# Squared-ReLU MLP jobs in pairs: products of two jobs alternate, quads kept twice, refill subtractions split between two engines

## What is computed

```python
hn = rms_norm(h, mlp_norm[i])
h = h + jnp.square(jax.nn.relu(hn @ w_mlp_in[i])) @ w_mlp_out[i]
```

## Time and profile before

| what | value |
|---|---|
| median of 3 runs | 2522.27 us (2521.65 to 2526.93) |
| the profiled execution's own time | 2522.98 us |
| its span, first to last instruction | 2521.2 us |
| granted TensorE clock, mean over the span | 0.966 |
| busy: TensorE, VectorE, GpSimd, ScalarE | 92%, 64%, 42%, 39% |
| MLP stages (line 1099) | from 542.9 and from 1699.4 us, some 675 us each |

### The profile page before, as it was taken

How to read it: one execution, slowest core, us unless ns; L and a number is a source line. 1 busy time by engine, 2 the same in 40 slices (tenths; PEclk the granted TensorE clock), 3 DMA queues, 4 the chain that set the end, 5 groups by cost and what they waited for, 6 DMA issues and landing times.

```text
span 2521.2 us, 31322 instructions
## 1 busy us (share of the span) xinstructions
PE 2321.1 (92%) x12286; PEld 1858.2 (74%) x12286; DVE 1611.7 (64%) x1959; ACT 980.9 (39%) x1526; POOL 1066.9 (42%) x684
## 2 busy tenths in 40 slices
PE   8998967997999989999998999987999989999997
PEld 6887856776888877777786776665888867877786
DVE  6867279558676766648627355567767676467725
ACT  3120255443444534433312245644444454334315
POOL 4433112234555545545332343634555545455421
PEclk9998978999999999999999999998999999999998
DMA  7372331212344634433113111111444464324111
GB/s 209 106 120 74 112 110 61 92 44 106 138 154 167 224 110 167 167 117 100 51 50 100 40 28 51 59 42 34 168 146 161 153 225 167 118 100 164 54 50 67
DMA packets 216867, 277.85 MB, mean 110 GB/s; under 512 B 32548, under 2 KB 171016, under 8 KB 212616
## 3 DMA queue, kind: packets, MB, share of 16 engines
q1 hardware_dynamic: 203176, 257.13, 30.5%
q10 hardware_dynamic: 13552, 18.81, 3.0%
...
## 4 chain that ended last, share of the span: by engine, by line
PE 71%; DVE 20%; ACT 4%; issue 3%; POOL 1%; ACTq 1%; DMA 0%; DVEq 0%; SPq 0%; POOLq 0%
PE ps L1099 39%; PE ps L727 15%; DVE op L2401 6%; PE ps L1265 3%; PE ps L878 2%; PE ps L1297 2%; DVE st_lo L2323 1%; PE ps L1225 1%; DVE hg_queries_keys L2166 1%; DVE residual L2387 1%; PE ps L1238 1%; PE ps L1249 1%; PE ps L899 1%; PE ps L914 1%; PE ps L794 1%
## 5 line engine op out<-in xcount | busy, mean ns | idle before, releaser
L1099 PE MATMUL ps<-op,st_hi 128*128 128x512 f32 x3584 | 1134.5, 398 | 93.1 <-DVE op L2401 39.3
L1099 PEld LDWEIGHTS ps<-op,st_hi 128*128 128x128 f32 x3584 | 683.1, 192 | 261.8 <-issue 100.3
L1099 PE MATMUL ps<-op,st_lo 128*128 128x512 f32 x1792 | 709.1, 396 | 0.0
L578 POOL TENSOR_TENSOR st_lo<-st_raw,st_hi 128x512 fp32r<-128x512 f32 x192 | 323.9, 1687 | 631.2 <-ACT st_hi L1348 631.2
L1099 PEld LDWEIGHTS ps<-op,st_lo 128*128 128x128 f32 x1792 | 343.5, 192 | 73.3
L1348 ACT ACTIVATE st_hi<-st_sum 128x512 fp32r<-128x512 f32 x256 | 160.3, 630 | 436.6 <-POOL st_sum L573 232.1
L557 POOL CAST w_hi<-w_raw 128x1024 fp32r<-128x1024 f32 x66 | 74.1, 1123 | 482.2 <-issue 249.3
L2387 DVE TENSOR_TENSOR residual<-residual,ps 128x512 f32<-128x512 f32 x192 | 131.3, 684 | 192.6 <-PE ps L1099 191.2
L1348 ACT ACTIVATE st_hi<-st_raw 128x512 fp32r<-128x512 f32 x192 | 120.6, 628 | 262.4 <-PE ps L1099 262.4
L573 POOL TENSOR_TENSOR st_sum<-st_raw 128x512 f32<-128x512 f32 x128 | 180.9, 1413 | 57.9 <-DVE st_lo L2323 57.9
L2323 DVE TENSOR_TENSOR st_lo<-st_sum,st_hi 128x512 fp32r<-128x512 f32 x256 | 193.9, 758 | 0.4
...
## 6 DMA issues: line engine op xcount, KB each, us to landing
mid_dram<-mid_sums SPq DMA_DIRECT2D x32, 1792.0 KB, 5.7
op_raw<-mid_dram SPq DMA_DIRECT2D x56, 1024.0 KB, 6.1
st_raw<-w_mlp_in_in SPq DMA_DIRECT2D x32, 1024.0 KB, 5.4
st_raw<-w_mlp_out_in SPq DMA_DIRECT2D x32, 1024.0 KB, 5.3
w_raw<-w_in_even_in SPq DMA_DIRECT2D x20, 512.0 KB, 4.5
...
w_raw<-w_ple_gate_in SPq DMA_DIRECT2D x16, 512.0 KB, 4.1
...
```

Source lines behind the costliest of these rows:

```text
L578: pool.tensor_tensor(SL[r][:, :, :], x, SH[r][:, :, :].bitcast(F32), sub).then_inc(S["st_lo_pool"], 1)
L1099: ins = pe.matmul(PS[:, o, :], w[:, j, :], OP[s][:, x, j, :], start=(s < 3 and j == 0 and w is SH[r] and x == 0), stop=(j == 3 and w is SL ...
```

## The change

**Order of products.** Jobs 2k and 2k+1 form a set. Within a set the products alternate: (2k, 0), (2k+1, 0), (2k, 1), (2k+1, 1) and so on, 14 in all; only the last set of an MLP keeps the old order. All engines' loops and all semaphore values follow the new numbering (k the set, r the place in it).

**Quads.** Q exists twice, by the parity of the job. Products 0 and 3 are copied by ScalarE into Q itself, evictions add in place, `p1` and the two `part` tiles are gone. Scaling is two operations of three operands that also apply the Relu (max with 0), for 1024 columns each; Square runs in place as one operation of 2048 columns. Three further sums go to `mid_sums` (two pieces, twice) and to one tile `mid_last_sum` (T4), and one is made in Q. A job is stored by three DMAs of 1024, 512 and 256 KB. The order of the pieces in `mid_dram` changes with it. ScalarE's copy into Q waits for the store of the job two before, and for its last sum; VectorE's last sum waits for the store of the T4 before.

**SA and SB** exist twice, too. GpSimd works a set at a time: first sum, low part 0 and second sum of each job, then low parts 3, the last sums, low parts 6.

**Weights' buffers.** st_raw has one buffer per parity as before, but both jobs of a set are in use at once; the load for the next set is issued once the job's low part 6 is made (r = 9 and 10).

**Refills.** The last set of a chunk gives a block free every second product. VectorE subtracts the first half of a block's low part, GpSimd the second; TensorE waits for the first at j = 0 and for the second at j = 2.

**Head.** The order of the late operands is changed, and GpSimd makes one of their subtractions (`late_operand`, 2048 columns). The down jobs' first copies into `p1_sum` are made by ScalarE.

The diff, cut to its core:

```diff
+IN_DRAM = (0, 5, 4, 1, 3, 2, 6)
+def product_at(n):
+    k, r = divmod(n, 2 * SLOTS)
+    b, s = divmod(r, SLOTS) if k == SETS - 1 else (r % 2, r // 2)
+    return 2 * k + b, s
...
+    Q = [at(f"quads{b}", [P, 4, HALF], F32, o) for b, o in enumerate((E1_AT, MISC_AT + 12 * K))]
+    MT = [at(f"mid_sums{b}", [P, 2, HALF], F32, E1_AT + (8 + 4 * b) * K) for b in range(2)]
+    T4 = at("mid_last_sum", [P, HALF], F32, E0_AT + 12 * K)
+    Z1 = [at(f"p1_sum{q}", [P, HALF], F32, E1_AT + (8 + 2 * q) * K) for q in range(4)]
...
+                def refill(c, s):
+                    sp.wait_ge(S["st_prod"], made(i, UP - 1 + 4 * c, s))
+                    if s == 0:
+                        for b in range(2):
+                            sp.wait_ge(*set_stored(i, 4 * c + 2 + b))
+                            sp.wait_ge(mt_stored[b], 16 * (UP // 2 * i + 2 * c + 2))
+                        sp.wait_ge(S["t4_stored"], 16 * (UP * i + 4 * c + 4))
+                    sp.dma_start(OPF[s][:, 1, :, :], t_dram[i][4 * c:4 * c + 4, :, IN_DRAM[s], :].rearrange("j p n -> p j n"))\
+                        .then_inc(x_op_loaded[s], 16)
+                def store_set(g):
+                    sp.wait_ge(S["q_ready"], UP * i + g + 1)
+                    sp.dma_start(t_dram[i][g][:, 0:4, :], Q[g % 2][:, :, :]).then_inc(stored[g % 2], 16)
+                def store_sums(g):
+                    sp.wait_ge(S["mt_ready"], UP * i + g + 1)
+                    sp.dma_start(t_dram[i][g][:, 4:6, :], MT[g % 2][:, :, :]).then_inc(mt_stored[g % 2], 16)
+                def store_last(g):
+                    sp.wait_ge(S["t4_ready"], UP * i + g + 1)
+                    sp.dma_start(t_dram[i][g][:, 6, :], T4[:, :]).then_inc(S["t4_stored"], 16)
...
+                    if k >= SETS // 2 and k % 2 == 0 and r == 0 and k < SETS - 1:
+                        refill((k - SETS // 2) // 2, 6)
+                    if k >= SETS // 2 - 1 and k % 2 and r and r % 2 == 0 and k < SETS - 1:
+                        refill((k - SETS // 2 + 1) // 2, r // 2 - 1)
+                    if 1 <= k <= SETS // 2:
+                        if r == 3:
+                            store_set(g - 2)
+                        if r == 4:
+                            store_set(g - 1)
+                            store_sums(g - 2)
+                            store_last(g - 2)
+                        if r == 5:
+                            store_sums(g - 1)
+                        if r == 6:
+                            store_last(g - 1)
+                    if r in (9, 10) and k < SETS - 1:
+                        b = r - 9
+                        sp.wait_ge(S["st_lo_pool"], low_pool(i, g + b, 6))
+                        raw(g + 2 + b)
...
+                def late_operand():
+                    pool.wait_ge(S["op_x_scaled"], X_SCALED * i + 10)
+                    pool.wait_ge(S["op_x_sum"], X_SUMS * i + 9)
+                    pool.wait_ge(S["op_ready"], READY * i + 12)
+                    pool.tensor_tensor(OPF[6][:, 1, :, :], OPF[6][:, 1, :, :], OP[1][:, 0, :, :].bitcast(F32), sub).then_inc(S["op_x_sum"], 1)
...
+                def refill(c, s):
+                    pool.wait_ge(S["op_cast"], CASTS * i + X_CASTS + 14 * c + 2 * s + 2)
+                    pool.tensor_tensor(OP[s][:, 1, 2:4, :], OPF[s][:, 1, 2:4, :], OP[s][:, 0, 2:4, :].bitcast(F32), sub)\
+                        .then_inc(S["op_x_sum"], 1)
+                for k in range(SETS - 1):
+                    before = k >= SETS // 2 - 1 and k % 2
+                    after, c = k >= SETS // 2 and k % 2 == 0, (k - SETS // 2 + 1) // 2
+                    for g in (2 * k, 2 * k + 1):
+                        first_sum(g)
+                        low(g, 0)
+                        second_sum(g)
+                    if after:
+                        refill(c, 3)
+                    for g in (2 * k, 2 * k + 1):
+                        low(g, 3)
+                    if after:
+                        refill(c, 4)
+                    if k == 0:
+                        late_operand()
+                    for g in (2 * k, 2 * k + 1):
+                        last_sums(g)
+                        if after:
+                            refill(c, 5 + g % 2)
+                    if before:
+                        refill(c, 0)
+                        refill(c, 1)
+                    for g in (2 * k, 2 * k + 1):
+                        low(g, 6)
+                    if before:
+                        refill(c, 2)
+                for g in (JOBS - 2, JOBS - 1):
+                    first_sum(g)
+                    low(g, 0)
+                    second_sum(g)
+                    low(g, 3)
+                    last_sums(g)
+                    low(g, 6)
...
+                        if (g, 0) in COPIES:
+                            pe.wait_ge(S["st_p1"], copied(i, g, 0))
...
+                        if j == 0:
+                            pe.wait_ge(S["op_ready"], n + X_READY + SLOTS * ((g - UP) // 4) + s + 1)
+                        if j == 2:
+                            pe.wait_ge(S["op_x_sum"], X_SUMS * i + 11 + SLOTS * ((g - UP) // 4) + s + 1)
+                for n in range(PRODUCTS):
+                    g, s = product_at(n)
                     a_, b_, c_ = BANKS[g % 2]
...
+                def copy(g, s):
+                    a_, b = BANKS[g % 2][0], g % 2
+                    act.wait_ge(S["st_prod"], made(i, g, s))
+                    if s == 3:
+                        fn(Q[b][:, 0, :], PS[:, a_, :], ACT.Copy).then_inc(S["st_p1"], 1)
+                    elif g < UP:
+                        if g >= 2:
+                            act.wait_ge(*set_stored(i, g - 2))
+                            act.wait_ge(S["t4_ready"], UP * i + g - 1)
+                        elif g == 1:
+                            act.wait_ge(S["ss_done"], norm + 1)
+                        fn(Q[b][:, 1, :], PS[:, a_, :], ACT.Copy).then_inc(S["st_p1"], 1)
+                    else:
+                        act.wait_ge(mt_stored[(g - UP) // 2], 16 * (UP // 2) * (i + 1))
+                        act.wait_ge(S["t4_ready"], UP * i + UP - 1 + (g - UP) // 2)
+                        fn(Z1[g - UP][:, :], PS[:, a_, :], ACT.Copy).then_inc(S["st_p1"], 1)
...
+                    act.wait_ge(S["q_scaled"], UP * i + g + 1)
+                    fn(Q[g % 2][:, :, :], Q[g % 2][:, :, :], ACT.Square).then_inc(S["q_squared"], 1)
...
                 high(6)
                 x_late(i, 6, 1)
                 high(7)
...
+                copy(0, 0)
+                cast_late(i, 4, 9, 9)
+                high(8)
+                copy(1, 0)
+                cast_late(i, 5, 9, 9)
+                high(9)
+                high(10)
+                copy(0, 3)
+                high(11)
+                copy(1, 3)
+                cast_late(i, 6, 10, 11)
+                high(12)
+                high(13)
+                for t in range(10, PRODUCTS + 1):
+                    k, r = divmod(t, 2 * SLOTS)
+                    g = 2 * k
                     if t + 4 < PRODUCTS:
                         high(t + 4)
...
+                    if t == 2 * SLOTS - 1:
                         act.wait_ge(S["rcp_done"], norm + 1)
                         fn(RSTD[:, :], RSTD[:, :], ACT.Sqrt).then_inc(S["rstd_done"], 1)
...
+                    if 1 <= k <= SETS // 2:
+                        if r == 0:
+                            squared(g - 2)
+                        if r == 2:
+                            squared(g - 1)
+                    if 1 <= k < SETS // 2 + 2:
+                        if r == 4:
+                            copy(g, 0)
+                        if r == 6:
+                            copy(g + 1, 0)
+                    if 1 <= k < SETS // 2:
+                        if r == 7:
+                            copy(g, 3)
+                        if r == 8:
...
+                    _, b_, c_ = BANKS[g % 2]
+                    q = Q[g % 2]
+                    dve.wait_ge(S["st_prod"], made(i, g, s))
+                    if s < 3:
+                        dve.wait_ge(S["st_p1"], copied(i, g, 0))
+                        tt(q[:, 4 - s, :], q[:, 1, :], PS[:, (b_, c_)[s - 1], :], add).then_inc(S["st_ev"], 1)
+                    elif s == 6:
+                        tt(q[:, 1, :], q[:, 1, :], PS[:, b_, :], add).then_inc(S["st_ev"], 1)
                     else:
...
+                        dve.wait_ge(S["st_ev"], ev(i, g, 6 - s))
+                        tt(q[:, s - 2, :], q[:, s - 2, :], PS[:, (b_, c_)[s - 4], :], add).then_inc(S["st_ev"], 1)
...
+                    for h, t in ((0, lefts), (2, rights)):
+                        ins = dve.scalar_tensor_tensor(q[:, h:h + 2, :], q[:, h:h + 2, :], 0.0, RSTD[:, t].unsqueeze(1).to_broadcast([P, 2, HALF]),
+                                                       ALU.max, ALU.mult)
+                    ins.then_inc(S["q_scaled"], 1)
+                def first_mid_sums(g):
```

(66 more changed lines are left out.)

370 lines of the change are left out of this document (140 added, 230 removed).

## The result

| | before | after |
|---|---|---|
| median, five runs each, same chip | 2522.27 us (2521.4 to 2526.93) | 2537.65 us (2534.48 to 2544.24) |
| ratio, 95% interval | | 1.0063 [1.0045, 1.0081] |
| profiled execution, its span | 2522.98, 2521.2 | 2537.65, 2535.9 |
| mean granted TensorE clock | 0.966 | 0.964 |

A forecast was written before the change was run, and what follows sets the result against it. Prediction: holes in the TensorE matmul stream, in the head and at down-phase refills, bound the kernel. Losses of 20 + 7.5 + 5 + 11 + 3 = 46.5 us per MLP replace 66.1, 39 less for both: 2484 us, range 2440 to 2540.

The forecast's parts named there:

- I leave 1 us for each of the last three refills, 3 us in all: Down phase: refills, split between VectorE and GpSimd, fit beside the matmuls and lose 3 us per MLP; ends 0 and 12.
- the 46.5 predicted: Loss per MLP after the change: 20 head, 7.5 up chain, 5 set 7, 11 set 8, 3 refills.
- 66.1: Predicted loss of one MLP before the change: 27.4 us in the head and 38.7 us in four refills.
- VectorE 2.5 of 2.72 us per product, GpSimd at most 27.1 of 38.1 us per pair: Down phase: work per product, VectorE's with a turn lost to GpSimd at each operation, and GpSimd's work per pair, both fitting.
- The third rival: Down phase: refills still bound through engine turns, 4 us in each of 7 sets, 28 for 3; 2534 us; chance 0.1.
- 27.1 + 8.4 us of GpSimd: Even down set: GpSimd's work plus turns lost to VectorE; with 4.3 us idle it makes 39.8 against 38.1 us.
- Sets 7 and 8: Last up set loses 5 us, stores sharing the queue with refill loads; first down set 11 us, ends 3 and 20.
- The up chain: Sets 2 to 6: quads' sums, store and ScalarE's copy come late, 1.5 us lost per pair, 7.5 us in all.
- The long chain: Rival: up chain loses 5 us and 2 of clock per pair in sets 2 to 7; 2549 us; chance 0.22.
- The head: Sets 0 and 1 of each MLP lose 20 us against 27.4 before; ends 14 and 26.
- the 2484 forecast for the whole: Whole kernel: 19.6 us less lost per MLP, 39 for both, from 2522.98 us; chance 0.5.

The follow-up runs named there:

- Experiment 1: After, with GpSimd's refill half 1 moved behind the pair's last low parts and half 2 into the next set: 2517.43 us, 0.9971 of before.
- experiment 2: After, with both halves of each refill on VectorE, one product later, none on GpSimd, pairs kept: 2493.08 us, 0.9871 of before.
- experiment 7: On experiment 5, the two further adds of each finished z put behind the low part of the same step: 2485.5 us, 0.9838 of before.
- experiment 11: On experiment 7 plus earlier weight casts and the head's subtraction on VectorE: set 8's square and set 14's z adds later; 2462.67 us, 0.9755 of before.
- experiment 5: After, with the changes of experiment 2 and experiment 4 together: 2488.34 us, 0.9842 of before.
- experiment 8: After, GpSimd keeping its halves, with the reorderings of Experiment 1 and experiment 4 together: 2509.32 us, 0.9937 of before.
- experiment 3: Before, jobs one by one, with GpSimd making the second half of each refilled block's low part: 2554.18 us, 1.0114 of before.
- experiment 4: After, with first job's last sums and stores of sums ahead of second job's, and one set 7 refill load behind those stores: 2527.86 us, 1.0006 of before.

## Why the prediction was wrong

**The step that failed is "I leave 1 us for each of the last three refills, 3 us in all".** Measured: 25.1 and 24.4 us in sets 9 to 15. This is 22 of the 31 us per MLP that separate the 46.5 predicted from the 77 measured (mean of both). Before's own loss was 71.6 in the mean and not 66.1: I took the end of the chain piece in the earlier trace rows, 1218.4, for the end of the MLP, whose last product ends at 1221.1, and the second MLP's head loses 6 us more. So 25 us per MLP, 50 for both, come through to the total, of the 53.7 us by which the forecast missed.

Three things were wrong in that step. First, it rested on shares: VectorE 2.5 of 2.72 us per product, GpSimd at most 27.1 of 38.1 us per pair. Over the down phase GpSimd's share looks like that (234.45 us of 355), but the mean hides the pairs: in sets 10 and 12, which have four of the seven halves, GpSimd was busy 34 to 35 us, since its instructions took longer beside VectorE's, and in sets 9 and 11 only 21 to 24 (GpSimd alone in windows of sets 10 and 12: length, busy us and count, clock, DMA share, GB/s):

```profile
972.30:1014.60 42.30, 34.26 (x20) 0.96 0.25 84
1054.40:1096.70 42.30, 35.21 (x21) 0.96 0.24 83
```

Second, an engine with room still delays others when its queue is in order and a waiting instruction stands ahead of one that is needed. I asked how much work GpSimd got and not what its new instructions wait for and what is queued behind them, though the diff shows refill half 1 ahead of the pair's last low parts. Experiment 1 prices that place at 20 us. Third, the count per product leaves out the further adds of each finished z on VectorE: with no half on GpSimd (experiment 2), slots 4 to 6 of set 14, where they stand, still lose 8.3 / 5.9 us. Moving them in experiments 7 and 11 won part of it.

**The third rival named the outcome.** It gave 28 us in place of 3 and 2534 us, and had 0.1. Its mechanism, the turns, is about half of the truth (21 us between experiments 5 and 8), and the order the other half; and the loss is not even over seven sets, as it put it, but falls on the boundaries to sets 10, 12 and 14 and on set 8. Its sum for a pair, 27.1 + 8.4 us of GpSimd, is what sets 10 and 12 show. The rule that I weighed before it, that of the Trainium skill (Perfetto Trace Analysis, Optimizing Scalar/DVE Operations) that offloading between these two might not help, is borne out here: experiments 2 and 3 on either side of before. I stated it and then priced VectorE's half at 1.2 us and GpSimd's at 2.4, their undisturbed durations; they took 1.68 and 2.83.

**Sets 7 and 8** lost 9.0 / 9.4 and 16.9 / 15.9 for 5 and 11. The mechanism of set 7 was right (the store of the last sum behind refill loads), its size was not: 4.75 us of hole, since the store took 7.7 us and stood behind the second job's quads as well; experiment 4 took 5 us of it away. In set 8 the copy of the first down product waited for the store of sums as forecast, with the turns of VectorE and GpSimd on top (the 5.65 us above).

**The up chain** was forecast at 1.5 us a pair and cost 0.6: the pairs in the windows above take 38.52 to 38.68 us for 38.1. The chain is there (ScalarE's copies are released late), the collisions that I placed one by one were fewer. The long chain, my main rival at 0.22, did not happen.

**The head** was right in the first MLP, 18.8 for 20, with the holes where I put them: slots 6 and 7 of set 0, the hole of GpSimd's 2048-column subtraction (4.61 us measured, 4.8 forecast). In the second MLP it lost 28.7. Before shows a difference of the same kind (27.2 and 33.2): I took the second MLP for a copy of the first, though its window in the earlier trace rows has the lower clock, 0.86. Since before loses 6 us more there too, this costs the comparison only some 3 us.

**What was right** is what the pairs do: experiment 2, the pairs without GpSimd's halves, measures 2493, 9 us from the 2484 forecast for the whole, and its down sets from 9 to 15 lose 9.8 / 7.4 where before lost 28.4. The change's gain was there; the part of it that I called neutral took it back.

Still open: why the second MLP's first set loses 4 to 7 us more than the first's in every kernel here, and whether set 8, the largest loss left, can be relieved by spreading VectorE's sums. Neither was tried.
